# Mixer heads: probabilities divided by VectorE before TensorE turns them, instead of outputs multiplied by turned reciprocals

## What is computed

```python
def hybrid_mixer(h, w_in, q_gain, k_gain, rel_bias, pool_w, pool_scale, w_out):
    proj = h @ w_in                        # 256 x 1024 @ 1024 x 2048: q, k, v, u of 512 columns each
    a = chunked_attention(q, k, v, q_gain, k_gain, rel_bias)
    p = multiscale_pool(u, pool_w, pool_scale)
    return jnp.concatenate([a, p], axis=-1) @ w_out

# in chunked_attention, for each head and chunk of 64 queries
s = einsum('bqhd,bkhd->bhqk', qb, kb) * scale + bias
p = softmax(where(valid, s, NEG_INF))
o = einsum('bhqk,bkhd->bqhd', p, vb)
```

## Time and profile before

| | |
|---|---|
| median of 3 runs | 703.39 us |
| the profiled execution | 703.74 us |
| its span (first to last instruction) | 701.9 us |
| TensorE busy | 692.2 us (99%) |
| VectorE busy | 529.3 us (75%) |
| ScalarE busy | 397.4 us (57%) |
| GpSimd busy | 98.2 us (14%) |
| mean DMA rate | 184 GB/s |
| TensorE's granted clock, mean over the span | 0.997 |

### The profile page before, as it was taken

The page is one execution under the profiler, slowest core; times in us unless marked ns, Lnnn a source line. Parts: engine busy times, 40 slices in busy tenths (PEclk is TensorE's granted clock), DMA queues, the critical chain, the costliest instruction groups (busy, mean ns, idle before and its releaser), DMA issues.

```text
span 701.9 us, 9837 instructions
## 1 busy us (share of the span) xinstructions
PE 692.2 (99%) x3716; PEld 590.1 (84%) x3716; DVE 529.3 (75%) x774; ACT 397.4 (57%) x536; POOL 98.2 (14%) x72
## 2 busy tenths in 40 slices
PE   8999999999999999999999999999999999999995
PEld 7888888888888788888888888888888888888884
DVE  6797779989876556876679989976762747898756
ACT  6865545576377656644555566487444625576441
POOL 0022204000001300022205000000007072140002
PEclk9999999999999999999999999999999999999998
DMA  9987552348465334754552438564763273543001
GB/s 342 359 347 262 197 194 98 142 154 322 138 263 202 120 99 150 261 181 180 183 197 102 176 122 329 210 252 169 239 242 115 82 285 134 170 161 130 1 1 60
DMA packets 21109, 129.34 MB, mean 184 GB/s; under 512 B 2504, under 2 KB 3664, under 8 KB 6864
## 3 DMA queue, kind: packets, MB, share of 16 engines
q1 hardware_dynamic: 19728, 127.51, 49.7%
q10 hardware_dynamic: 1344, 1.34, 0.6%
HBM read 127.79 MB, written 1.06 MB: 184 GB/s over the span
## 4 chain that ended last, share of the span: by engine, by line
PE 97%; DVE 1%; DMA 1%; ACT 0%; SPq 0%; issue 0%; POOL 0%; POOLq 0%; DVEq 0%
PE ps L502 24%; PE ps L467 16%; PE ps L469 15%; PE ps L468 15%; PE ps L508 13%; PE ps L487 1%; PE ps L762 1%; DMA raw<-in_first 1%; PE ps L661 1%; PE ps L1114 1%; PE ps L933 1%; PE ps L521 1%; PE ps L491 1%; PE ps L817 1%; PE ps L818 1%; PE ps L819 1%
## 5 line engine op out<-in xcount | busy, mean ns | idle before, releaser
L1671 DVE TENSOR_TENSOR wlo<-raw,whi 128x2048 fp32r<-128x2048 f32 (+1 forms) x77 | 173.7, 2267 | 23.9 <-ACT whi L1191 23.7
L1191 ACT ACTIVATE whi<-raw 128x2048 fp32r<-128x2048 f32 (+1 forms) x86 | 161.3, 1879 | 40.5 <-PE ps L469 37.3
L502 PE MATMUL ps<-xt,whi 128*128 128x512 f32 x752 | 180.1, 391 | 0.0
L502 PEld LDWEIGHTS ps<-xt,whi 128*128 128x128 f32 x752 | 138.1, 188 | 26.7
L467 PE MATMUL ps<-whi,xt 128*128 128x512 f32 (+2 forms) x340 | 135.0, 397 | 0.1
L469 PE MATMUL ps<-whi,xt 128*128 128x512 f32 (+2 forms) x340 | 130.1, 383 | 0.0
L468 PE MATMUL ps<-wlo,xt 128*128 128x512 f32 (+2 forms) x340 | 129.9, 382 | 0.0
L508 PEld LDWEIGHTS ps<-xt,wlo 128*128 128x128 f32 x752 | 96.4, 191 | 3.7
L508 PE MATMUL ps<-xt,wlo 128*128 128x256 f32 x752 | 97.5, 283 | 0.0
L1594 POOL TENSOR_TENSOR wlo<-raw,whi 128x2048 fp32r<-128x2048 f32 (+1 forms) x9 | 41.0, 4558 | 290.1 <-ACT whi L1191 290.1
L1754 DVE TENSOR_TENSOR wlo<-raw,whi 128x2048 fp32r<-128x2048 f32 x32 | 75.7, 2366 | 1.2
(11 more groups left out here) (259 smaller groups left out, 776.8 us busy)
## 6 DMA issues: line engine op xcount, KB each, us to landing
raw<-in_gu SPq DMA_DIRECT2D x41, 1024.0 KB, 4.8
raw<-in_dn SPq DMA_DIRECT2D x22, 1024.0 KB, 4.7
raw<-in_win SPq DMA_DIRECT2D x8, 1024.0 KB, 4.8
raw<-in_fqk SPq DMA_DIRECT2D x8, 1024.0 KB, 4.8
raw<-in_wout SPq DMA_DIRECT2D x4, 1024.0 KB, 5.4
raw<-in_fg SPq DMA_DIRECT2D x4, 1024.0 KB, 7.3
raw<-in_fv SPq DMA_DIRECT2D x4, 1024.0 KB, 4.7
raw<-in_fo SPq DMA_DIRECT2D x4, 1024.0 KB, 4.8
```

Source lines behind the costliest of these rows:

```text
L502: return pe.matmul(ps[:, banks[u], :], wh[:, k * S + u * P:k * S + (u + 1) * P], x, start=k == 0, stop=k == KD - 1)
L1191: act.activation(whi[:, c % RING, w], raw[:, c % RING, w], ACT.Copy).then_inc(hi_ready, 1)
L1671: dve.tensor_tensor(wlo[:, c % RING, w], raw[:, c % RING, w], whi[:, c % RING, w].bitcast(F32), ALU.subtract).then_inc(lo_ready, 1)
```

## The change

The reciprocals are no longer turned. VectorE takes the reciprocals of one head's sums, a new `divide(h)`, and multiplies the head's probabilities in place in `probs1` by them, in two instructions (128 and 256 columns), before TensorE turns them. `turn_probs` of these heads waits for that (`probs_divided`) and no longer for the exponentials. `turn_rinv`, `spread_rinv`, `row_of_rinv` and `divided` are gone, and the outputs in the bank are final: `outputs_hi` and `outputs_lo` read the banks. VectorE's order of the heads is written anew.

```diff
--- before.py
+++ after.py
@@ -216,9 +216,6 @@
         part_sum = view(work, NG * S, BANK)
 
         qkn = XN[:, :, :].rearrange("p t (n c) -> p n t c", n=2)
-        attn1 = view(XN[:, 0, :], 0, 1024, "p (k s) -> p k s", k=4)
-        rinv_rows = view(XN[:, 1, :], 0, 512, "p (b s) -> p b s", b=2)
-        rinv_wide = view(XN[:, 1, :], 512, 512, "p (b t h d) -> p b t h d", b=2, t=NT, h=2)
         sq = view(work, 0, 2048, "p (n t c) -> p n t c", n=2, t=NT)
         q1t = view(work, 0, 1024, "p (k s) -> p k s", k=4)
         k1t = view(work, 1024, 1024, "p (k s) -> p k s", k=4)
@@ -309,7 +306,7 @@
         s_psum, neg_ready, exp_done, pt_psum, pt_ready, pv_psum = (
             [sem(f"{n}_{i}") for i in range(3)] for n in ("s_psum", "neg_ready", "exp_done", "pt_psum", "pt_ready", "pv_psum"))
         rinv_ready, a_done = [sem(f"rinv_ready_{i}") for i in range(3)], [sem(f"a_done_{i}") for i in range(3)]
-        rinv_spread, rinv_turned, rinv_row = sem("rinv_spread"), sem("rinv_turned"), sem("rinv_row")
+        probs_divided = sem("probs_divided")
         at_psum, at_hi, at_lo = sem("at_psum"), sem("at_hi"), sem("at_lo")
         y_psum_t, y_hi, y_lo = sem("y_psum_t"), sem("y_hi"), sem("y_lo")
 
@@ -757,7 +754,10 @@
             def turn_probs(i, h, bank):
 
                 src = [probs1, probs2, probs3][i]
-                pe.wait_ge(exp_done[i], 2 * h + 2)
+                if i:
+                    pe.wait_ge(exp_done[i], 2 * h + 2)
+                else:
+                    pe.wait_ge(probs_divided, 2 * h + 2)
                 for b in range(3):
                     m = pe.transpose(ps[:, bank, b * P:(b + 1) * P], src[:, h % 2, b * P:(b + 1) * P], ident)
                 m.then_inc(pt_psum[i], 1)
@@ -822,22 +822,13 @@
 
                 pe.wait_ge(pt_ready[0], 2 * pair + 2)
                 if pair >= 2:
-                    pe.wait_ge(a_done[0], pair - 1)
+                    pe.wait_ge(at_lo, 1)
                 heads = [(slice(DH1 * i, DH1 * (i + 1)), i, slice(DH1 * (2 * pair + i), DH1 * (2 * pair + i + 1))) for i in range(2)]
                 for rows, i, d in heads:
                     pe.matmul(ps[rows, pair % 2, 0:S], v1[:, 0, d], pt1[:, i, 0:S], start=True, stop=False)
                 for rows, i, d in heads:
                     m = pe.matmul(ps[rows, pair % 2, P:S], v1[:, 1, d], pt1[:, i, S:S + P], start=False, stop=True)
                 m.then_inc(pv_psum[0], 1)
-
-            def turn_rinv(pair):
-
-                pe.wait_ge(rinv_spread, pair + 1)
-                if pair >= 2:
-                    pe.wait_ge(a_done[0], pair - 1)
-                for t in range(NT):
-                    m = pe.transpose(ps[:, pair % 2, S + t * P:S + (t + 1) * P], rinv_wide[:, pair % 2, t, :, :].rearrange("p h d -> p (h d)"), ident)
-                m.then_inc(rinv_turned, 1)
 
             u_step(0)
             scores1(0)
@@ -847,7 +838,6 @@
                     if h % 2 and h >= 3:
                         scores1((h + 1) // 2)
                         values1((h - 3) // 2)
-                        turn_rinv((h - 3) // 2)
                     u_step(h + 1)
                 else:
                     values1(2)
@@ -859,7 +849,6 @@
                         m = pe.matmul(o[:, P:S], u_sb[:, 1, g * P:(g + 1) * P], band[:, g, S:S + P], start=False, stop=True, skip_group_check=True)
                         if g % 2:
                             m.then_inc(d_psum, 1)
-                    turn_rinv(2)
                 if h >= 2:
                     pe.wait_ge(pt_ready[0], h - 1)
                 turn_probs(0, h, 6 + h % 2)
@@ -882,7 +871,6 @@
             pe.wait_ge(neg_ready[0], 2 * H1)
             attention_out(0, 0)
             values1(H1 // 2 - 1)
-            turn_rinv(H1 // 2 - 1)
 
             for g in range(4):
                 pe.wait_ge(d_act if g // 2 else d_dve, 1)
@@ -1313,25 +1301,10 @@
                     act.wait_ge(at_psum, n + j - 1)
                     act.activation(h[:, k0 + 2 * j:k0 + 2 * j + 2, :], ps[:, b, :].rearrange("p (k s) -> p k s", k=2), ACT.Copy).then_inc(at_hi, 1)
 
-            def spread_rinv(pair):
-
-                act.wait_ge(rinv_ready[0], pair + 1)
-                if pair >= 2:
-                    act.wait_ge(rinv_turned, pair - 1)
-                act.activation(rinv_wide[:, pair % 2, :, :, :], rinv[:, 2 * pair:2 * pair + 2, :].rearrange("p h t -> p t h").unsqueeze(3).broadcast_to([P, NT, 2, DH1]),
-                               ACT.Copy).then_inc(rinv_spread, 1)
-
-            def row_of_rinv(pair):
-
-                act.wait_ge(rinv_turned, pair + 1)
-                if pair >= 2:
-                    act.wait_ge(a_done[0], pair - 1)
-                act.activation(rinv_rows[:, pair % 2, :], ps[:, pair % 2, S:2 * S], ACT.Copy).then_inc(rinv_row, 1)
-
             def outputs_hi(half):
 
-                act.wait_ge(a_done[0], 2 * half + 2)
-                act.activation(a1h[:, 2 * half:2 * half + 2, :], attn1[:, 2 * half:2 * half + 2, :], ACT.Copy).then_inc(at_hi, 1)
+                act.wait_ge(pv_psum[0], 2 * half + 2)
+                act.activation(a1h[:, 2 * half:2 * half + 2, :], ps[:, 0:2, 0:S], ACT.Copy).then_inc(at_hi, 1)
 
             def part_high(c, cols, part, landed, src):
 
@@ -1381,22 +1354,16 @@
                                scale=sm[:, SM_GK:SM_GK + 1]).then_inc(k1_ready, 1)
             hi(C_WIN + 5 + RING)
             for h in range(H1):
+                if h == 6:
+                    outputs_hi(0)
                 exps(0, h)
                 if h == 3:
                     hi(C_WIN + 6 + RING)
                 if h == 6:
                     act.wait_ge(chunk_used, C_WIN + 8)
                     act.activation(u_sb[:, 0, :], ps[:, 2, :], ACT.Copy, scale=rstd[:, 0:1]).then_inc(u_ready, 1)
-                if h % 2 == 0 and h >= 2:
-                    spread_rinv(h // 2 - 1)
-                if h % 2 and h >= 3:
-                    row_of_rinv(h // 2 - 1)
-                if h == 6:
-                    outputs_hi(0)
             act.wait_ge(d_psum, 2)
             act.activation(d_t[:, 2:4, :].rearrange("p g s -> p (g s)"), ps[:, 3, :], ACT.Copy).then_inc(d_act, 1)
-            spread_rinv(3)
-            row_of_rinv(3)
             outputs_hi(1)
             for g in range(4):
                 act.wait_ge(y_psum, g // 2 + 1)
@@ -1895,42 +1862,49 @@
                 dve.tensor_scalar(q1t[:, 2 * b:2 * b + 2, :].rearrange("p k s -> p (k s)"), ps[:, b, :], sm[:, SM_GQ:SM_GQ + 1], SCALE1, ALU.mult, ALU.mult).then_inc(q1_ready, 1)
             dve.wait_ge(par_landed, 16)
 
-            def rinv_of(pair):
-
-                dve.wait_ge(exp_done[0], 4 * pair + 4)
-                heads = slice(2 * pair, 2 * pair + 2)
-                dve.reciprocal(rinv[:, heads, :], sums[:, heads, :]).then_inc(rinv_ready[0], 1)
-
-            def divided(pair):
-
-                dve.wait_ge(pv_psum[0], pair + 1)
-                dve.wait_ge(rinv_row, pair + 1)
-                dve.tensor_tensor(attn1[:, pair, :], ps[:, pair % 2, 0:S], rinv_rows[:, pair % 2, :], ALU.mult).then_inc(a_done[0], 1)
+            def divide(h):
+
+                dve.wait_ge(exp_done[0], 2 * h + 2)
+                dve.reciprocal(rinv[:, h, :], sums[:, h, :]).then_inc(rinv_ready[0], 1)
+                dve.wait_ge(rinv_ready[0], h + 1)
+                for t in range(NT):
+                    p = probs1[:, h % 2, COL[t]:COL[t] + KEYS[t]]
+                    dve.tensor_scalar(p, p, rinv[:, h, t:t + 1], None, ALU.mult).then_inc(probs_divided, 1)
 
             def outputs_lo(half):
 
                 dve.wait_ge(at_hi, half + 1)
                 k = slice(2 * half, 2 * half + 2)
-                dve.tensor_tensor(a1l[:, k, :], attn1[:, k, :], a1h[:, k, :].bitcast(F32), ALU.subtract).then_inc(at_lo, 1)
-
-            for h in range(H1):
+                dve.tensor_tensor(a1l[:, k, :], ps[:, 0:2, 0:S], a1h[:, k, :].bitcast(F32), ALU.subtract).then_inc(at_lo, 1)
+
+            def shares(h):
+
                 masked(0, h, lambda t: bias1[:, h, P:2 * P] if t == 0 else bias1[:, h, :], SCORES1[h // 2])
+
+            def turned(h):
+
+                probs_out(0, h, 6 + h % 2)
+
+            shares(0)
+            shares(1)
+            divide(0)
+            divide(1)
+            turned(0)
+            shares(2)
+            turned(1)
+            divide(2)
+            for h in range(3, H1):
+                shares(h)
+                if h == 6:
+                    outputs_lo(0)
                 if h == H1 - 1:
                     dve.wait_ge(chunk_used, C_WIN + 8)
                     dve.tensor_scalar(u_sb[:, 1, :], ps[:, 3, :], rstd[:, 1:2], None, ALU.mult).then_inc(u_ready, 1)
-                if h >= 1:
-                    probs_out(0, h - 1, 6 + (h - 1) % 2)
-                if h % 2 == 0 and h >= 2:
-                    rinv_of(h // 2 - 1)
-                if h in (4, 6):
-                    divided(h // 2 - 2)
-            outputs_lo(0)
-            rinv_of(3)
```

(6 more changed lines are left out.)

## The result

The changed kernel takes 712.35 us, the median of 4 runs (712.04 to 712.98), against 703.77 us for the kernel before (4 runs, 703.12 to 704.21): a ratio of 1.012, with a 95% interval of 1.0103 to 1.0136. It is 8.6 us slower; the forecast was 709.9 us, with a range of 706.6 to 712.9. The profiled execution is the one of 712.04 us, with a span of 710.2 us (703.74 and 701.9 before).

What follows compares the result with a forecast made beforehand. TensorE was taken to bound the kernel (97% of the chain of waits). Steps of +3.75, +0.1, +2.9, +0.6 and +0.05 less 0.9 gave +6.5 us on 703.74, 710.2; less 0.35, 709.9 us, range 706.6 to 712.9.

Steps and rivals of the forecast that it cites:

- the clock rival: TensorE's clock also falls in the first wait, slowing later products by up to 3.5 us: 710 to 713.4 us, chance 0.08.
- the likeliest case: The forecast itself, divisions of heads 0 and 4 both held by GpSimd: 709.0 to 711.0 us, chance 0.73.
- Removed, -0.9: Four `turn_rinv` leave TensorE's path, 0.9 us (0.8 to 1.1); the work removed from ScalarE and VectorE wins nothing.
- What holds the multiplication: VectorE's multiplication by a scalar moves two columns a step, so it stands until GpSimd's instruction ends.
- Step 1: Head 0: both multiplications run behind GpSimd's first conversion, ending 230.31; turning at 230.95 instead of 227.21, +3.75 us.
- Step 2: Head 2: its division, behind head 0's copy on VectorE, ends at 234.4 to 234.5, wanted at 234.39; +0.1 us.
- Step 3: Head 4: its division meets GpSimd's second conversion (237.5 to 242.1); turning at 242.7 instead of 239.8, +2.9 us.
- Step 4: `scores1(3)` waits for head 5's `masked`, behind head 4's division and head 3's copy on VectorE; +0.6 us.
- Step 5: Later heads: divisions ready 0.5 us or more before turning, VectorE's u part still before head 7's division; +0.05 us.
- The sum without the clock: All steps and the removal together, TensorE's clock staying up: +6.5 us.
- nothing held: Rival: the multiplication does not need GpSimd's way into SBUF, 703.1 us (702.5 to 704.3), chance 0.14.
- only one held: Rival: only head 0's division is held, head 4's escapes GpSimd's second conversion; 706.6 us, chance 0.05.

Runs made afterwards that it cites:

- undivided: Changed kernel without the division: no reciprocals or multiplications on VectorE, probabilities turned as the exponentials leave them; 702.78 us against 703.59.
- one_port: Changed kernel, each multiplication also sums its row into an unused column, so it moves one column a step; 704.42 us against 703.59.
- two_inputs: Changed kernel, each multiplication by a scalar written as a product of two SBUF operands; 712.76 us in a single run.
- pool_late: Changed kernel, GpSimd's two conversions wait until the last head is divided; 703.70 us against 703.59.
- busy_pe: Changed kernel, TensorE makes 13 products of idle data before turning head 0 and 8 before head 4; 710.00 us against 703.59.
- reordered: Changed kernel, both GpSimd conversions late, ScalarE's high part of C_WOUT+1 behind head 1's exponentials, head 5's `masked` before head 3's copy; 703.44 us against 703.39.
- by_parts: Changed kernel, both GpSimd conversions late, head 5's `masked` before head 3's copy, reciprocal and multiplication made part by part; 703.52 us against 703.50.
- second_late: Changed kernel, only GpSimd's second conversion waits until the last head is divided; 707.35 us against 703.39.
- hold_alone: Kernel before, plus one VectorE multiplication of 128 idle columns by a scalar ahead of head 0's copy, no division; 704.99 us against 703.39.

## Why the prediction was right or wrong

The direction, the mechanism of the hold and its two places were right, and the time lies inside the range, 0.55 us under its upper end. It does so because the range took in half of the clock rival: the likeliest case's own range, 709.0 to 711.0, was missed. The number was 2.45 us low. Of this 0.38 is the kernel before, which measured 703.77 beside the changed one and not 703.39; the other 2.1 are the clock, 2.4 in the heads and on top of the rest, twice, less 0.2 to 0.3 by which the other steps together were priced too high.

- **What bounds the kernel**: right. All that TensorE lost is in the result.
- **Removed, -0.9**: 0.83 (undivided). That nothing else was won was right too.
- **What holds the multiplication**: right. The slopes named the form, and one_port and two_inputs together show it. A division outside GpSimd's instructions takes 0.17 + 0.55 us less the overlap, as priced.
- **Step 1, +3.75**: +3.43 (6.44 for 3.01). I had both multiplications run behind GpSimd's end, 0.54; the pair ended 0.34 after it, since the first is through 0.08 us after GpSimd and only the second, 0.34 long, comes wholly behind.
- **Step 2, +0.1**: +0.23 over heads 1 and 2 where the clock stays up (3.67 in pool_late for 3.44).
- **Step 3, +2.9**: +2.64 in busy_pe, +2.29 in the changed kernel, where the slow stretch had moved the conversion. The second conversion was forecast from 237.5 and began at 237.95 (at 237.13 in busy_pe, where the clock stayed up); head 4's division met it in the same way.
- **Step 4, +0.6**: the scores start 0.93 after head 4's turning, for 0.42: +0.5, and +0.6 in busy_pe (1.02). The cause is the one that reordered and by_parts take away where nothing is held (0.17 us there).
- **Step 5**, small waits of +0.05: none ahead of head 7's turning in the changed kernel (3.20 us from head 6's, 3.19 in undivided), 0.13 in pool_late (3.32), where the pooling's first product starts 0.47 us after the outputs' last ones, 0.32 in the changed kernel: it waits a little for VectorE's part of u, which ends at 243.11 there.
- **The sum without the clock**: forecast +6.5, measured +6.26 in the heads of busy_pe.
- **The clock**: the step that failed. I took the idle time at the end of the span, some 3.6 us before the clock was down, for what it takes, gave the first wait a small chance of it and the second, of 2.9 us, none. The clock fell behind both, though TensorE idled only 2.13 us in the second; its price of up to 3.5 us for one fall holds what was measured (1.42 for the first alone, 2.4 for both), but as a bound only. So what I took from the span's end, that it needs an idle time about that long, is what the runs contradict. The two rivals on the other side, nothing held and only one held, did not come about; pool_late and second_late are what they would have looked like: 703.7 where I had 703.1, and 707.35 where I had 706.6 (there the clock came on top, behind the first wait).

## What to carry to other kernels

Before an instruction is moved to VectorE, look at what GpSimd does at that time and at how the new instruction reaches SBUF: if it moves two columns a step, or has two operands in SBUF, it may stand for the rest of GpSimd's instruction, here 3.8 us for one of 0.28, and everything behind it on VectorE with it. A slower form (here the multiplication that also sums, 0.35 for 0.29 us) takes 7.9 of the 8.6 us away, a conversion moved elsewhere all of them. But the change had 0.8 us to win at best, and no version of it beat the kernel before. And price a long wait of TensorE with the slow stretch that may come with it: here 1.1 to 1.4 us for each, and in two_inputs some 2.5 (6.67 us from head 4's turning to head 5's, 4.17 in busy_pe).

## What the runs showed of the hardware

- A held instruction is shown busy while it stands: VectorE's busy time rose from 529.3 to 539.0 us, and the two held pairs are 6.93 us of it. Long rows of an instruction that is short elsewhere are the sign.
- How long TensorE idled did not decide alone whether its clock fell. In the changed kernel it fell behind waits of 3.28 and 2.13 us; in two_inputs it stayed at 1.00 behind a wait of 3.41 us and fell at the next one, of 2.73 us. In hold_alone, at 1.41 us, it stayed. When it fell in the changed kernel, it did so not in the wait but about 1 us (first) and 2 us (second) after the work had begun again, and came back some 3.4 us later. In two_inputs it fell in the wait, at 242.5 for a turning that starts at 242.71, and was down for 6.8 us. Why a longer wait leaves it up and a shorter one brings it down, and why one slow stretch is twice as long as the other, stays open; no run here separates that.
